# A decoder step on one core: order of the first products, and the thin gate and decay product in four column groups

## The reference

```python
mod = (jax.nn.silu(c) @ w_ada + b_ada)[:, None, :]      # c: 1 prompt row and 8 sample rows
sh1, sc1, gt1, sh2, sc2, gt2 = jnp.split(mod, 6, axis=-1)
h = rmsnorm(x, g_mix) * (1 + sc1) + sh1
qa, ka, va, fa, qb, kb, vb, rb, alr, ga, gb = split_cols(h @ w_in, IN_SIZES)
logf = jax.nn.log_sigmoid((fa + b_f).astype(jnp.float32))          # fa: 8 columns
log_a = jax.nn.log_sigmoid((alr @ w_alpha + b_alpha)...) / GLA_TAU # alr: 16 columns
```

## Time and profile before

| | |
|---|---|
| median of 3 runs | 1245.64 us (1245.16 to 1246.57) |
| the profiled execution, own time | 1247.54 us |
| its span, first to last instruction | 1245.7 us |
| TensorE matmuls busy | 1163.0 us, 93% |
| VectorE, ScalarE busy | 328.1 us, 176.0 us |
| mean DMA rate | 402 GB/s, 500.76 MB |

### The profile page before, as it was taken

The page is one execution under the profiler, slowest core; times in us unless marked ns, Lnnn a source line. Parts: engine busy times, 40 slices in busy tenths (PEclk is TensorE's granted clock), DMA queues, the critical chain, the costliest instruction groups (busy, mean ns, idle before and its releaser), DMA issues.

```text
span 1245.7 us, 15292 instructions
## 1 busy us (share of the span) xinstructions
PE 1163.0 (93%) x6044; PEld 583.8 (47%) x6044; DVE 328.1 (26%) x685; ACT 176.0 (14%) x348; POOL 48.2 (4%) x95
## 2 busy tenths in 40 slices
PE   7999999999999999898989989998998988899997
PEld 4788756688543443434343435344242424243333
DVE  3289975323221020111101111111021011103123
ACT  3133232200211100200020011002000200020102
POOL 1032122100000000000000000000000000000000
PEclk9999999999999999999999998999999999999999
DMA  9998999999799999999999999999999999999995
GB/s 341 358 370 312 377 355 372 405 406 369 295 406 429 428 427 427 429 429 428 428 429 418 428 427 404 429 428 428 426 428 428 428 429 428 429 428 428 421 417 207
DMA packets 72700, 500.76 MB, mean 402 GB/s; under 512 B 9049, under 2 KB 11171, under 8 KB 43836
## 3 DMA queue, kind: packets, MB, share of 16 engines
q1 hardware_dynamic: 65840, 478.38, 93.2%
q0 software_dynamic: 6576, 21.42, 4.8%
q10 hardware_dynamic: 220, 0.09, 0.0%
HBM read 496.48 MB, written 3.38 MB: 401 GB/s over the span
## 4 chain that ended last, share of the span: by engine, by line
PE 69%; DMA 24%; DVE 2%; ACT 2%; issue 1%; SPq 1%; DVEq 0%
PE ps L1083 23%; DMA ring<-in_w_d 16%; PE ps L520 12%; PE ps L1170 11%; DMA early<-in_w_d 8%; PE ps L1267 4%; PE ps L1024 4%; PE ps L425 3%; PE ps L869 2%; PE ps L934 2%; PE ps L967 2%; PE ps L477 1%; SPq L2548 1%; ACT oT L1583 1%; PE ps L1040 1%
## 5 line engine op out<-in xcount | busy, mean ns | idle before, releaser
L1083 PE MATMUL ps<-ring,zone 128*64 128x512 f32 x1488 | 414.2, 593 | 6.6 <-DMA ring<-in_w_gu 2.8
L1170 PE MATMUL ps<-ring,oT 128*64 128x512 f32 x784 | 237.5, 617 | 31.3 <-DMA ring<-in_w_d 18.2
L1083 PEld LDWEIGHTS ps<-ring,zone 128*64 128x64 f32 x1488 | 132.4, 137 | 221.6 <-issue 218.1
L520 PE MATMUL ps<-early,ring 128*128 128x264 f32 x640 | 150.7, 392 | 2.3 <-DVE early L1748 1.4
L2211 DVE TENSOR_SCALAR zone<-ps 128x1024 f32<-128x1024 f32 x14 | 17.1, 1224 | 477.8 <-PE ps L1083 455.4
L1170 PEld LDWEIGHTS ps<-ring,oT 128*64 128x64 f32 x784 | 72.8, 142 | 148.5 <-issue 125.2
L520 PEld LDWEIGHTS ps<-early,ring 128*128 128x128 f32 x640 | 120.5, 192 | 31.2 <-issue 8.9
L1083 PE MATMUL ps<-zone 128*64 128x512 f32 x284 | 114.8, 593 | 0.0
L1083 PE MATMUL ps<-early,zone 128*64 128x512 f32 x240 | 98.8, 593 | 0.0
L1560 ACT ACTIVATE ps<-zone 128x1024 f32<-128x1024 f32 x14 | 14.4, 1027 | 450.9 <-DVE zone L2211 450.9
L1083 PEld LDWEIGHTS ps<-zone 128*64 128x64 f32 x284 | 35.4, 137 | 75.0 <-issue 74.1
(11 more groups left out here) (405 smaller groups left out, 957.5 us busy)
## 6 DMA issues: line engine op xcount, KB each, us to landing
ring<-in_w_gu SPq DMA_DIRECT2D x93, 2048.0 KB, 26.9
ring<-in_w_d SPq DMA_DIRECT2D x45, 2048.0 KB, 22.2
zone<-in_w_gu SPq DMA_DIRECT2D x16, 2048.0 KB, 25.3
early<-in_w_gu SPq DMA_DIRECT2D x15, 2048.0 KB, 31.2
ring<-in_w_ada SPq DMA_DIRECT2D x12, 2048.0 KB, 12.3
ring<-in_w_in SPq DMA_DIRECT2D x18, 1024.0 KB, 11.5
early<-in_w_d SPq DMA_DIRECT2D x8, 2048.0 KB, 24.3
zone<-in_w_d SPq DMA_DIRECT2D x7, 2048.0 KB, 19.6
```

What stands on the lines that cost most here:

```text
L520: ins = pe.matmul(bank[0:width, 0:T], w[:, k, c0:c0 + width], hT[:, k, :], start=(k == 0), stop=(k == KT - 1))
L1083: ins = pe.matmul(ps[64 * j:64 * j + CAP, c, :], xg[:, k, 2 * par + j, :], rows, start=False, stop=(k == KT - 1), skip_group_check=True)
L1170: ins = pe.matmul(ps[64 * j:64 * j + CAP, 4 + c, :], hidT[:, k, j * CAP:(j + 1) * CAP], w[j][:, kk, c * 512:(c + 1) * 512], start=(k == 0) ...
```

## The change

SyncE issues `ada0` ahead of the tokens. ScalarE applies Silu to the conditioning rows directly behind their two loads and issues the other ten loads after it. TensorE turns the conditioning first, multiplies `ada0`, and then turns all eight token tiles in a row. VectorE copies `cT` first, then tiles 0 to 5, scales the sums (`x_var`), copies tiles 6 and 7, and then takes the reciprocal and the diagonals. The thin product puts even contraction tiles into rows 0 and 32 and odd ones into rows 64 and 96 of the bank, and VectorE adds the two halves.

```diff
-            pe.wait_ge(sig("x_tok"), 32)
-            turn_tokens(range(4))
             pe.wait_ge(sig("c_silu"), 1)
             bank = vector_bank()
             for k in range(KT):
                 ins = transpose(bank[:, 9 * k:9 * k + 9], c_rows[:, k * P:(k + 1) * P])
             vector_filled(ins, "cT")
-            turn_tokens(range(4, 6))
...
             from_vector("cT")
             modulate_half(0, 0)
-            turn_tokens(range(6, KT))
+            pe.wait_ge(sig("x_tok"), 32)
+            turn_tokens(range(KT))
...
             for k in range(KT):
-                pe.matmul(bank[0:HA, 0:T], w_f[:, k, :], hT[:, k, :], start=(k == 0), stop=(k == KT - 1),
+                row = 64 * (k % 2)
+                pe.matmul(bank[row:row + HA, 0:T], w_f[:, k, :], hT[:, k, :], start=(k < 2), stop=(k >= KT - 2),
                           skip_group_check=True)
-                ins = pe.matmul(bank[32:48, 0:T], w_alr[:, k, :], hT[:, k, :], start=(k == 0), stop=(k == KT - 1),
-                                skip_group_check=True)
+                ins = pe.matmul(bank[row + 32:row + 48, 0:T], w_alr[:, k, :], hT[:, k, :], start=(k < 2),
+                                stop=(k >= KT - 2), skip_group_check=True)
...
             dma(c_rows[1:9, :], c_sample, "c_rows")
+            act.wait_ge(sig("c_rows"), 32)
+            nc.scalar.activation(c_rows, c_rows, ACT.Silu).then_inc(sig("c_silu"), 1)
...
-            act.wait_ge(sig("c_rows"), 32)
-            nc.scalar.activation(c_rows, c_rows, ACT.Silu).then_inc(sig("c_silu"), 1)
...
-            take_tokens(range(4))
             give(V.tensor_copy(cT[:, :, 0:9], take("cT")[:, 0:9 * KT].rearrange("p (k c) -> p k c", c=9)), "cT")
-            take_tokens(range(4, 6))
+            take_tokens(range(6))
 
             dve.wait_ge(sig("ssq"), 3)
             V.tensor_scalar(rstd, ssq, 1.0 / D, EPS, ALU.mult, ALU.add).then_inc(sig("x_var"), 1)
+            take_tokens(range(6, KT))
...
             ins.then_inc(sig("rstd_diag"), 1)
-            take_tokens(range(6, KT))
...
                 bank = take("falr")
-                V.tensor_copy(alrT, bank[32:48, 0:T]).then_inc(sig("alrT"), 1)
-                give(V.tensor_scalar(fT, bank[0:HA, 0:T], b_f_col[:, 0:1], None, ALU.add), "falr", then_read=True)
+                V.tensor_copy(fT, bank[64:64 + HA, 0:T])
+                chain(V.tensor_copy(alrT, bank[96:112, 0:T]))
+                V.tensor_tensor(alrT, bank[32:48, 0:T], alrT, ALU.add).then_inc(sig("alrT"), 1)
+                give(V.scalar_tensor_tensor(out=fT, in0=bank[0:HA, 0:T], scalar=b_f_col[:, 0:1], in1=fT,
+                                            op0=ALU.add, op1=ALU.add), "falr", then_read=True)
...
-            sp.dma_start(tok[:, 0:2, :], x_prompt[0].rearrange("(t p) d -> p t d", p=P)).then_inc(sig("x_tok"), 16)
-            sp.dma_start(tok[0:NS, 2, :], x_sample.rearrange("b s d -> (b s) d")).then_inc(sig("x_tok"), 16)
             for item in ITEMS:
                 load(item)
+                if item == "ada0":
+                    sp.dma_start(tok[:, 0:2, :], x_prompt[0].rearrange("(t p) d -> p t d", p=P)).then_inc(sig("x_tok"), 16)
+                    sp.dma_start(tok[0:NS, 2, :], x_sample.rearrange("b s d -> (b s) d")).then_inc(sig("x_tok"), 16)
```

## The result

| | before | after |
|---|---|---|
| median of 20 runs each | 1246.54 us | 1250.15 us |
| ratio after/before, 95% interval | | 1.0028 [1.0019, 1.0037] |
| profiled execution, span | 1245.7 us | 1249.2 us |

The change made the kernel slower by 0.28%, 3.6 us between the medians. The prediction (1244.4 us, range 1242.0 to 1247.0) was wrong in sign and outside its range. The trace shows one gain and one loss: the thin product is 1.8 us shorter, and the first query tile starts 4.95 us later.

A forecast was written before the change was run, and what follows sets the result against it. The prediction took TensorE's work before the last DMA restart at 331 us as the bound, carried one for one to the end. Front +0.45 and thin product -1.7 gave -1.25 us: median 1244.4, range 1242.0 to 1247.0.

The forecast's parts named there:

- The tile's price and the pace: Front, eight token tiles from 13.1 us: one slow at 0.85, pace doubling near 13.9, seven at 0.5, end 17.4.
- the stretch at 318 us: Sixteen turns from 317.6 us, granted clock 0.80 over 5 us, cited as evidence against turns lowering the clock.
- rival 2: Front: clock stays or falls low behind eight token turns; 1246.8 tiles alone (0.12), 1249.7 with both products (0.07).
- The two products behind: Behind the token tiles, the diagonals' product and ada1's product would keep their 1.02 and 1.93 us.
- the strong form of rival 2: Front: tiles at 0.85, diagonals' and ada1's products also at the low level; +4.1 us, 1249.7, chance 0.07.
- point of decision: Front: rival 2 would be decided by whether the tokens' end passes 21 us.
- The bound: Front: TensorE works without a wait from 7.05 to 21.5 us; only an earlier start or better clock shortens it.
- rival 1: Front gains too: tokens land near 11.3, clock stays up through the first query tiles; -3.3 us, 1242.3, chance 0.20.
- The hidden chain: Front: reciprocal and diagonals behind VectorE's last copies, 17.4 + 0.43 + 1.18 = 19.0, where the diagonals' product starts.
- The tokens' landing: Front: tokens land behind ada0, not before 11.0 nor later than 12.7 us, taken as 12.3.
- the gain of the thin product: Gate and decay columns near 56 us: four column groups take 1.79 us, gaining 1.78; -1.7 stays on the path.
- One for one: Whatever TensorE gains or loses before the last DMA restart at 331 us comes out unchanged at the end.

The follow-up runs named there:

- after_warm: The changed kernel plus seven products of ones on TensorE before the conditioning's turns; ratio to the kernel before 1.0026 [1.0013, 1.0038].
- after_filled: The changed kernel plus three products of ones before the conditioning and two between ada0's product and the wait for the tokens; ratio to before 1.0014 [1.0001, 1.0027].
- after_matmul_turns: The changed kernel with token tiles turned by ordinary products with the identity instead of transpose mode; ratio to the kernel before 1.0043 [1.0026, 1.0061].
- after_kept_up: `after_filled` plus products of ones behind token tiles 1, 3, 5, before the diagonals' product and around the turn of ada1's result; ratio to before 1.0004 [0.9989, 1.002].

## Why the prediction was wrong

**The tile's price and the pace.** The step that failed: "With the same delay it doubles near 13.9: one slow tile, then seven at 0.5, end at 17.4." The tiles took 0.85 us each, all eight, and ended at 13.32 + 6.84 = 20.16. Three things were wrong in it. The pace did not rise 4.4 us after the first dense product began at 9.51; I had carried a delay read once over to a place where 6.8 us of turns stand behind that product. Where the pace was up (`after_warm`, `after_filled`), a row of turns let it fall again, and with ordinary products in their place it stayed up (`after_matmul_turns`). And a tile at the upper pace costs 0.65 us, not 0.5: I had taken the copy's 0.43 as its floor, but TensorE sets it. Of the 2.8 us between 17.4 and 20.16, 7 x 0.35 = 2.45 are this step, 1.4 of them the pace and 1.05 the price of 0.5; the rest is nearly all the later start.

The Trainium skill ("TensorE: Matmul & The Clock Gate", Part 4) says that a turn in transpose mode doesn't count as busy the way a product does. This case's traces agree. The cleanest pair is `after_warm`, whose turns in transpose mode stand at a granted clock of 0.60 and then 0.50, and `after_matmul_turns`, whose turns by ordinary products keep 1.00. `after_filled` and `after_kept_up` say the same by the last two copies, 0.85 and 0.65 us apart; their diagonals' products (1.74 and 0.76 us) differ also by the two products of ones in the wait just before, so they prove less.

I had set against it the stretch at 318 us, where "the clock is back behind them". That was a misreading of a mean over 5 us. Cut finer, the trace of the kernel before says the opposite:

```profile
315.00:318.00 3.00, 3.00 (x27) 2.57 (x27) 1.05 (x5) 1.62 (x3) 0.00 (x0) 1.00 0.94 369
318.00:321.00 3.00, 3.00 (x19) 2.67 (x20) 2.53 (x18) 2.13 (x4) 0.00 (x0) 0.50 1.01 426
```

The sixteen turns run from 317.58 to 320.90. TensorE is busy all the time, and yet the granted clock is 0.50 from 318.0 on and comes back only from 321.4, within the products behind them. The fall begins 0.4 us into the turns, so the small products ahead of them may have a part in it; but the row spoke for rival 2, against which the forecast had used it.

**The two products behind.** "Behind it everything is as before: 1.02, ada1's product 1.93". They took 1.74 and 2.96, 1.75 us more. This is the strong form of rival 2, which I gave 0.07, at 1249.7 us with +4.1; the medians say +3.6. Its form was right, its size a little high, since the pace came back within `ada1`'s product (2.96, not 3.64). Its point of decision was wrong, and at odds with the forecast's own bound (eight tiles at 0.85 end at 19.9): the tiles ended at 20.16, not past 21.

**The bound.** "Only a start before 7.05 or a better clock could shorten it", with a lower bound of -1.2 us for the front and rival 1 beside it at 0.20. Both ignored a row that I had: `ada1` lands at 19.1 and its product started at 19.52. By the forecast's own "ada1 stays where it is, at 19.1" that left 0.4 us. I read "TensorE works without a wait" as "TensorE is the bound", but it was busy and just in time. The statement on `ada1` was wrong too, by luck without effect: it landed near 18.2, so 1.3 us were there to gain, but its product started only at 23.44. Either way the change had less to gain in the front than the 2.9 us that the forecast's own upper bound gave it to lose.

**The hidden chain.** In the old order the root, the reciprocal and the diagonals ended at 15.03, hidden by `ada0`'s product. In the new one the reciprocal stands behind the last copy. I had seen this, and its price was right: 20.16 + 0.43 + 1.18 = 21.77, where the diagonals' product starts, with a wait of 1.03 on TensorE.

**The tokens' landing.** "Not later than 12.7" gave 13.27. I had counted the bytes of `ada0` and the tokens alone, 3.18 MB. The changed kernel's DMA engines move 305 GB/s on average up to 13.27 us, which is 4.05 MB, so some 0.9 MB of other loads came in beside them. `ada1` and `qa` are issued right behind; how much of it is theirs wasn't measured. It is 1.0 us against the 12.3 that I took, of which 0.2 reached TensorE, which was at `ada0`'s product until 9.51 + 3.64 = 13.15.

**What was right.** Silu behind its two loads, the small loads at no cost, `ada0` at 9.3 (forecast 9.5), the gain of the thin product (1.77 measured in the trace, 1.78 forecast; its length is 1.90 for the 1.79 of the forecast, whose own 16 / 2 x 0.22 is 1.76), VectorE's sums hidden, and the waits before the first query tile. One for one holds to about a microsecond: the scores are 3.17 us later than before, the restart of the loads 4.26, the end 3.5. The restart came at 336.07 for the 330.5 forecast; 4.5 of these 5.6 us are the front, and the rest was lost behind the first scores.

## What to carry to other kernels

An engine that is busy without a gap is not yet the bound: put the landing of each load beside the start of the work that uses it, and the smallest distance is what a reordering of the engine's work can gain while the loads stay as they are. Turns are cheap work to hide under a load, and dear work in a row: here neither they nor the products behind them kept the upper pace until something stood between them. Filling the gaps with useless products brought the pace back, but not the time of the old order with the same thin product. A delay of the clock read at one place holds only for the work around that place, and a mean clock over a stretch longer than the work in question can hide where it fell.

## What the runs showed of the hardware

The granted clock of a stretch doesn't carry the level at the start of an execution. In the changed kernel it reads 1.00 from 7 to 13 us, where 32 records of `ada0`'s product take 3.64 us and the same form takes 1.93 later:

```profile
7.00:13.00 6.00, 4.48 (x40) 2.31 (x40) 0.23 (x1) 0.97 (x1) 0.00 (x0) 1.00 1.03 381
```

The trace's clock records begin with the first rise (12.72 us in `after_matmul_turns`, 17.62 in the kernel before, 25.56 in the changed kernel); ahead of it every stretch reads 1.00. The durations of a repeated form are the safer reading there. And for float32, eight token tiles turned by ordinary products took 8.0 us (0.99 a tile) at the upper level, in transpose mode 5.3 us for the most part at the upper and 6.8 at the low one.
